# Modulation sums of a three-block transformer kernel: one-hot stationary operand in four column groups, rows turned once a layer

## The chip, the cores and the metric

The kernel runs on one core of one Trainium2 chip. The metric is device time in microseconds (us) of one launch. The engines are TensorE (PE, its weight loads PEld), VectorE (DVE), ScalarE (ACT), GpSimd (POOL) and SyncE (SP), which here only issues weight loads. Everything is float32.

## The reference, cut to what matters

Two transformer layers over 256 tokens and 256 context tokens, then a third block with a mixture of experts. Each of the three layers has a modulation: one or two condition vectors (`c` and `c_ctx` in layers 0 and 1, `c_2` in the third) times a 1024 x 6144 matrix give six vectors that shift, scale and gate the layer.

```python
def modulation(cvec, w, b):
    m = jax.nn.silu(cvec) @ w + b
    return jnp.split(m[..., None, :], 6, axis=-1)
...
        sh1, sc1, g1, sh2, sc2, g2 = modulation(c, w_mod[i], b_mod[i])
        csh1, csc1, cg1, csh2, csc2, cg2 = modulation(c_ctx, w_mod[i], b_mod[i])
        h = x * (1.0 + sc1) + sh1
        hc = xc * (1.0 + csc1) + csh1
```

## The kernel before

Weights come in pieces of 1024 x 512 (2 MB) through a ring of four slots, `wring`, that SP fills in the fixed order `STREAM`; piece i waits until piece i-4 is released. PSUM is eight banks, given out in turn by `claim(name)`: claim i waits until the bank of claim i-8 was freed, and `moved(name)` is the wait for that. Each engine has its own instruction stream, written out by hand, with semaphores between them.

A modulation matrix is 12 chunks of 512 columns, `("mod0", m)` to `("mod2", m)`. The first four chunks of layer 0 are needed at once: `mod_rows` multiplies them on TensorE with the two condition vectors as a stationary operand of two columns, giving rows 2 x 512, which ACT copies to SBUF (`modrow`) and TensorE turns into columns. The eight matmuls of such a chunk accumulate over its eight row blocks k.

The other 32 chunks are spread over the program (`BESIDE`): 8 of layer 0 beside the first projection `ev_in`, 12 of layer 1 and 2 of layer 2 beside the first layer's up projection `up0`, 10 of layer 2 beside `up1`. For such a chunk DVE (`sum_mods`) adds the eight row blocks, each scaled by its entry of the condition vector, into one 128 x 512 tile for each vector; 16 operations with two vectors, 8 with one. What remains is a sum over the 128 partitions. TensorE takes it: a block of 128 x 128 of that tile is the stationary operand, a column of ones the moving one, and the result is a column of 128 values. That is four matmuls for each vector, 208 in all. They stand singly between the matmuls of a `features` or `tokens` call (`take_sum`), one ahead of each of its 128x512 or 128x256 matmuls. ACT copies the 4 or 8 columns to `modc` (`mods`), and `finish_mod` adds the bias on DVE before the layer that needs them.

In the MLP (`mlp`) each block c of `up` is four features of eight matmuls; ACT takes the relu, DVE the square, and DVE sums a chunk after every second square. A chunk summed in block c is taken by TensorE in block c+1, ahead of feature 0 or 2 (`due`).

Every float32 matmul leaves two records in the trace, each with its own weight load; a transpose leaves one. Counts below are of records.

Of the kernel before, what the change touches and what calls it, by code (L numbers as in the profile page):

```python
# [13 lines left out]
P = 128  # L14
# [29 lines left out]
def _place(names):  # L44
    at = 0
    for name, width in names:
# [7 lines left out]
                  ("ones", 1), ("before", P), ("home", NEXP), ("spill", NEXP), ("expert", NEXP), ("turn", SPILLS),  # L54
# [5 lines left out]
def shape_constants():  # L60
# [31 lines left out]
    put("ones", 1.0)  # L92
    put("before", r < t)
# [71 lines left out]
ATT_BANKS = (5, 6, 0, 1, 2, 3, 7, 4)  # L165
# [25 lines left out]
def build(nc, I, out):  # L191
# [10 lines left out]
    with ExitStack() as ctx:  # L202
# [18 lines left out]
        small = sb("small", [P, 592])  # L221
        slot_i = sb("slot_i", [P, 4], I32)
# [37 lines left out]
        modsums = region(tmp, 2560, 2, 2, 512)  # L260

        def modsum(n, v):

            return gtok[:, 2 * (n % 2) + v, 512:D] if SUMMED[n][0] == 0 else modsums[:, n % 2, v, :]

# [173 lines left out]
        csilu_ready = sem("csilu_ready")  # L439
        modc_ready = sem("modc_ready")  # L440
# [110 lines left out]
        def _(pe):  # L551
# [41 lines left out]
            def open_sums(chunk):  # L593

                if chunk is None:
                    return []
                l, m = chunk
                V = vectors(l)
# [51 lines left out]
            def features(name, w, f, lo, hi, chunk=None):  # L650

                sums = open_sums(chunk)
                o = claim(name)
                for k in range(KC):
                    take_sum(sums, k)
# [3 lines left out]
            def tokens(name, w, t, width=512, at=0, chunk=None):  # L659

                sums = open_sums(chunk)
                o = claim(name)
                for k in range(KC):
                    take_sum(sums, k)
# [26 lines left out]
            def mlp(l, tiles):  # L691
                lo = 0
                n = len(tiles) * P
                for c in range(8):
# [3 lines left out]
                    release((f"up{l}", c))  # L698
                for half in range(2):
                    outs = [claim(f"down{l}{half}{t}") for t in tiles]  # L700
                    for g in range(4):
                        w = weights((f"down{l}", 4 * half + g))
                        if half == 0 and g == 0:
                            pe.wait_ge(*moved(f"up{l}31"))
# [103 lines left out]
            def take_alone(chunk):  # L808
                sums = open_sums(chunk)
                for k in range(len(sums)):  # L810
                    take_sum(sums, k)

            for n, c in enumerate(EV_ORDER):
# [7 lines left out]
                elif n == 2:  # L821
                    sums = open_sums(EV_TAKES[(2, 0)])
                    o = claim("lr0")
                    for k in range(KC):
                        take_sum(sums, k)
                        last = mm(o[0:32, :], w[:, k, 0:32], hT[:, k, :], k == 0, k == KC - 1)
                    last.then_inc(bank_full, 1)
                else:
                    for t in range(NT):
# [3 lines left out]
                        if (n, t) == (3, 0):  # L833
                            take_alone(EV_TAKES[(2, 1)])
# [11 lines left out]
                if n < 3:  # L846
                    release(("ev_in", n))
            for t in range(NT):
# [60 lines left out]
            assert count[0] % BANKS == ATT_BANKS[0]  # L909
# [527 lines left out]
        def _(act):  # L1437
# [70 lines left out]
            def mods(chunk):  # L1508

                if chunk is not None:  # L1510
                    l, m = chunk
                    V = vectors(l)
                    move(f"mod{l}_{m}", modc[:, l, 4 * m:4 * m + 4, 0:V],
                         bank(f"mod{l}_{m}")[:, 0:4 * V].rearrange("p (f v) -> p f v", v=V))

# [5 lines left out]
            def relus(l, n):  # L1521

                for i in range(32):
                    mods(due(f"up{l}", i // 4, i % 4))
# [4 lines left out]
            for c in range(4):  # L1529
                move(f"modrow{c}", modrow[0:2, c, :], bank(f"modrow{c}")[0:2, :])  # L1530
# [965 lines left out]
```

## Time and profile before

| | us |
|---|---|
| median of 3 runs (lowest to highest) | 1859.06 (1856.77 to 1860.87) |
| profiled execution, its own time | 1862.66 |
| its span, first to last instruction | 1860.8 |
| PE busy | 1703.6 |
| PE weight loads busy | 908.8 |
| DVE busy | 719.4 |
| ACT busy | 251.4 |

PE is busy in 92% of the span. Weight loads overlap with matmuls, so the two PE rows don't add. A matmul's recorded length includes its way through the pipeline; what it costs the stream is the distance of one start to the next.

### The profile page before, as it was taken

To read this page: it belongs to the slowest core of one execution; us is meant where nothing else is said; L and a number is where in the kernel's file an instruction comes from. 1 tells how busy PE (TensorE), PEld (TensorE's weight loads), DVE (VectorE), ACT (ScalarE), POOL (GpSimd) and SP (SyncE) were. 2 spreads that over 40 slices of the span, in tenths; PEclk is the share of its full clock that TensorE was granted. 3 is DMA by queue.
4 is the path that set the end of the run, shared out by engine and by line. 5 is a ranking of instruction groups with operands and counts; after the bars stand their busy time and mean duration, and the time that the engine had idled before them with its cause. 6 is when DMAs were issued, how large, how long until landed. Compare 5 with 4: busy or idle time off the path is not lost.

```text
span 1860.8 us, 16741 instructions
## 1 busy us (share of the span) xinstructions
PE 1703.6 (92%) x6670; PEld 908.8 (49%) x6670; DVE 719.4 (39%) x1292; ACT 251.4 (14%) x588; POOL 114.0 (6%) x121
## 2 busy tenths in 40 slices
PE   6999999899999999998898999997986675999997
PEld 1445556355554444445564886444744643333332
DVE  0654453557775001023373563012368633111112
ACT  1112113020000000001171110001201311110110
POOL 0000001100000000001000000002022101010001
PEclk9999999999999999999999999998998686999999
DMA  9452150225555322125303687433522127999996
GB/s 348 168 213 91 59 179 26 89 95 200 206 201 205 112 91 91 45 91 220 136 1 113 229 320 276 170 136 79 181 91 92 56 97 282 391 388 390 391 390 253
DMA packets 160685, 334.46 MB, mean 180 GB/s; under 512 B 15192, under 2 KB 15472, under 8 KB 160608
## 3 DMA queue, kind: packets, MB, share of 16 engines
q1 hardware_dynamic: 141408, 298.87, 44.4%
q0 software_dynamic: 18288, 31.37, 5.2%
q10 hardware_dynamic: 912, 3.17, 0.4%
q8 instruction: 53, 0.87, 0.2%
q14 instruction: 24, 0.20, 0.0%
HBM read 355.58 MB, written 15.48 MB: 199 GB/s over the span
## 4 chain that ended last, share of the span: by engine, by line
PE 84%; DVE 9%; DMA 2%; issue 2%; POOL 1%; ACT 1%; SPq 0%; DVEq 0%; ACTq 0%; POOLq 0%
PE psum L570 80%; PE psum L574 4%; POOL small L1329 1%; DMA wring<-in_w_mod 1%; DMA wring<-in_ev_w_in 1%; ACT wide L1460 1%; DVE big L2039 0%; DVE big L1813 0%; DVE small L1880 0%; ACT big L1460 0%; DVE xres L1887 0%; DVE big L2206 0%; DVE big L2225 0%; DVE small L2224 0%; DVE wide L2276 0%
## 5 line engine op out<-in xcount | busy, mean ns | idle before, releaser
L570 PE MATMUL psum<-wring,big 128*128 128x512 f32 (+1 forms) x1536 | 563.4, 603 | 13.5 <-issue 10.2
L570 PE MATMUL psum<-wide,wring 128*128 128x256 f32 (+3 forms) x1648 | 516.5, 478 | 3.5 <-DVE wide L1851 3.5
L570 PEld LDWEIGHTS psum<-wring,big 128*128 128x128 f32 (+1 forms) x1536 | 232.2, 174 | 327.8 <-issue 327.0
L570 PEld LDWEIGHTS psum<-wide,wring 128*128 128x128 f32 (+2 forms) x1648 | 269.2, 182 | 134.3 <-issue 109.0
L570 PE MATMUL psum<-wring,wide 128*128 128x512 f32 (+2 forms) x512 | 210.9, 561 | 3.4 <-DMA wring<-in_ev_w_in 3.4
L1813 DVE SCALAR_TENSOR_TENSOR wide<-wring,csilu,wide 128x512 f32<-128x512 f32 x252 | 175.5, 748 | 3.0
L1865 DVE TENSOR_TENSOR wide<-psum,gate 128x512 f32<-128x512 f32 x28 | 19.4, 691 | 356.7 <-PE psum L570 356.5
L1460 ACT ACTIVATE big<-psum 128x512 f32<-128x512 f32 (+1 forms) x153 | 79.9, 534 | 450.2 <-PE psum L570 394.4
L570 PEld LDWEIGHTS psum<-wring,wide 128*128 128x128 f32 x512 | 92.8, 193 | 89.2 <-issue 83.0
L1329 POOL TENSOR_TENSOR small<-small 128x1 f32<-128x1 f32 (+2 forms) x30 | 40.0, 1334 | 1117.6 <-DVE small L1882 926.6
L570 PE MATMUL psum<-big,wide 128*64 128x512 f32 (+1 forms) x408 | 91.7, 569 | 0.0
L1913 DVE TENSOR_TENSOR big<-big,psum 128x512 f32<-128x512 f32 (+1 forms) x64 | 35.3, 551 | 141.4 <-ACT big L1460 140.9
L570 PEld LDWEIGHTS psum<-const,wide 128*128 128x128 f32 x352 | 62.2, 190 | 55.9 <-issue 53.4
L570 PE MATMUL psum<-big 128*64 128x128 f32 (+5 forms) x608 | 71.2, 348 | 18.0 <-DVE big L2297 7.3
L1460 ACT ACTIVATE wide<-psum 128x256 f32<-128x256 f32 (+3 forms) x108 | 43.3, 415 | 314.3 <-PE psum L574 153.4
L2453 DVE TENSOR_TENSOR wide<-wide,psum 128x256 f32<-128x256 f32 x23 | 9.7, 421 | 180.4 <-ACT wide L1460 180.4
L1813 DVE SCALAR_TENSOR_TENSOR big<-wring,csilu,big 128x512 f32<-128x512 f32 x112 | 74.9, 745 | 0.0
L570 PEld LDWEIGHTS psum<-big 64*128 64x128 f32 (+2 forms) x608 | 51.6, 183 | 26.3 <-issue 13.8
L1460 ACT ACTIVATE wide<-psum,modc 128x256 f32<-128x256 f32 x36 | 18.4, 560 | 325.1 <-PE psum L574 323.5
L574 PE MATMUL psum<-const,wide 128*128 128x128 f32 (+1 forms) x238 | 40.7, 312 | 19.7 <-DVE wide L1905 16.5
L574 PEld LDWEIGHTS psum<-const,wide 128*128 128x128 f32 (+1 forms) x238 | 30.0, 160 | 54.1 <-issue 26.0
L570 PEld LDWEIGHTS psum<-big,wide 128*64 128x64 f32 (+1 forms) x408 | 31.7, 145 | 49.2 <-issue 48.3
(257 smaller groups left out, 1058.5 us busy)
## 6 DMA issues: line engine op xcount, KB each, us to landing
wring<-in_mlp_w SPq DMA_DIRECT2D x32, 2048.0 KB, 8.8
wring<-in_w SPq DMA_DIRECT2D x32, 2048.0 KB, 20.8
wring<-in_w_mod SPq DMA_DIRECT2D x24, 2048.0 KB, 11.9
big<-in_w SPq DMA_DIRECT2D x23, 2048.0 KB, 20.8
wide<-in_w SPq DMA_DIRECT2D x14, 2048.0 KB
wring<-in_w_ada SPq DMA_DIRECT2D x12, 2048.0 KB, 9.2
wring<-in_w_in SPq DMA_DIRECT2D x8, 2048.0 KB, 8.3
wring<-in_ev_w_in SPq DMA_DIRECT2D x6, 2048.0 KB, 13.1
```

The lines of the kernel that those rows point to most:

```text
L570: return nc.tensor.matmul(o, a, b, start=first, stop=last)
L574: return nc.tensor.transpose(o, a, ident[0:n, 0:n])
L1329: nc.gpsimd.tensor_tensor(a, a, half_neg[:, 0:a.shape[1]], ALU.pow).then_inc(rate_done, 1)
L1460: return nc.scalar.activation(o, a, func, **kw)
L1813: ins = v_.scalar_tensor_tensor(acc, w, by, acc, ALU.mult, ALU.add)
L1865: free(v_.tensor_tensor(ubuf, bank(name), gate[:, gv, cs], ALU.mult), name)
L1913: free(v_.tensor_tensor(h, h, bank(name)[:, 0:n], ALU.mult), name)
L2453: v_.tensor_tensor(he[:, i % 2, :], sg[:, i % 2, :], psum[:, i % 2, T:2 * T], ALU.mult).then_inc(he_ready, 1)
```

## The change

The 208 matmuls swap their operands. The stationary operand is now 32 columns of a constant `row`, 63 columns wide with ones in column 31 only, cut so that the ones stand in column m; the moving one is the 128 x 128 block. The result is a row of 128 values in row m of a group of 32 rows, zeros in the other 31; block f goes to row group 32f, so the four blocks of a vector use four column groups of the array. The matmuls of a chunk stand together ahead of the feature (`sum_rows`). DVE adds the 128 x 256 (or 128 x 128) result into a tile of rows of its layer (`add_row`, in place of ACT's copy), and when the layer's last chunk is in, `turn_rows` turns the tile with one matmul for each vector. `finish_mod` adds the bias straight from PSUM.

`mod_rows` is split into four column groups as well: eight row blocks k go to groups k mod 4, with a stationary operand `vec32` of 32 columns (two vectors and zeros), and the turning matmul with the constant `quarter` adds the four groups. PE claims one bank more for each layer, and `ATT_BANKS` is set to fit.

```diff
             def mod_rows():
-                vec = csilu[:, 0:16].rearrange("p (v k) -> p k v", v=2)
+                pe.wait_ge(vec32_ready, 1)
                 for c in range(4):
                     w = weights(("mod0", c))
                     o = claim(f"modrow{c}")
-                    for k in range(KC):
-                        last = mm(o[0:2, :], vec[:, k, :], w[:, k, :], k == 0, k == KC - 1)
+                    for n in range(KC // 4):
+                        for q in range(4):
+                            k = 4 * n + q
+                            last = mm(o[32 * q:32 * (q + 1), :], vec32[:, k, :], w[:, k, :], n == 0, n == KC // 4 - 1)
                     last.then_inc(bank_full, 1)
                     release(("mod0", c))
                 for c in range(4):
                     pe.wait_ge(*moved(f"modrow{c}"))
                     o = claim(f"mod0_{c}")
                     for f in range(4):
-                        last = turn(o[:, 2 * f:2 * f + 2], modrow[0:2, c, f * P:(f + 1) * P])
+                        last = mm(o[:, 2 * f:2 * f + 2], modrow[:, c, f * P:(f + 1) * P], cst("quarter"))
                     last.then_inc(bank_full, 1)
...
-                return [(o[:, f * V + v:f * V + v + 1], modsum(n, v)[:, f * P:(f + 1) * P])
-                        for f in range(4) for v in range(V)]
-
-            def take_sum(sums, k):
-
-                if k < len(sums):
-                    last = mm(sums[k][0], sums[k][1], cst("ones"))
-                    if k == len(sums) - 1:
-                        last.then_inc(bank_full, 1)
+                at = CONST_COLS["row"][0] + 31 - m
+                for v in range(vectors(l)):
+                    for f in range(4):
+                        last = mm(o[32 * f:32 * (f + 1), v * P:(v + 1) * P], const[:, at:at + 32],
+                                  modsum(n, v)[:, f * P:(f + 1) * P])
+                last.then_inc(bank_full, 1)
+
+            def turn_rows(l):
+
+                pe.wait_ge(rows_added, last_row(l))
+                o = claim(f"modT{l}")
+                for v in range(vectors(l)):
+                    last = mm(o[:, v * P:(v + 1) * P], rows_of_layer(l)[:, v, :], ident)
+                last.then_inc(bank_full, 1)
...
+                pe.wait_ge(*moved(f"up{l}31"))
+                turn_rows(l + 1)
                 for half in range(2):
                     outs = [claim(f"down{l}{half}{t}") for t in tiles]
...
+            turn_rows(0)
             for t in range(NT):
                 if t + 1 < NT:
                     scores(t + 1)
...
+            def add_row(chunk):
+
+                l, m = chunk
+                V = vectors(l)
+                name = f"mod{l}_{m}"
+                rows, src = rows_of_layer(l), ready(name)[:, 0:V * P].rearrange("p (v n) -> p v n", v=V)
+                n = SUMMED.index(chunk)
+                if n > 0:
+                    dve.wait_ge(rows_added, n)
+                if chunk == next(x for x in SUMMED if x[0] == l):
+                    ins = v_.tensor_copy(rows, src)
+                else:
+                    ins = v_.tensor_tensor(rows, rows, src, ALU.add)
+                free(ins, name)
+                dve.sem_inc(rows_added, 1)
...
                 for i in range(32):
                     name = f"up{l}{i}"
+                    if due(f"up{l}", i // 4, i % 4) is not None:
+                        add_row(due(f"up{l}", i // 4, i % 4))
                     dve.wait_ge(relu_ready, 32 * l + i + 1)
...
+            signal(v_.memset(vec32, 0.0), vec32_zero)
+            dve.wait_ge(csilu_ready, 1)
+            v_.tensor_copy(vec32[:, :, 0:2], csilu[:, 0:16].rearrange("p (v k) -> p k v", v=2)).then_inc(vec32_ready, 1)
             mods(0, 0, 4)
```

What stands in PE's stream at the start, `mod_rows` between the first two transposes of constants and the transposes of x; before:

```order
L574 MATMUL psum<-const,big 128x96 x2
L570 MATMUL psum<-wring,csilu 2x512 x32
L574 MATMUL psum<-const,wide 128x2 x16
L574 MATMUL psum<-const,xres 128x128 x32
L570 MATMUL psum<-wide,wring 128x512 x32
```

and of the change:

```order
L589 MATMUL psum<-const,big 128x96 x2
L585 MATMUL psum<-wring,wide 32x512 x32
L585 MATMUL psum<-const,wide 128x2 x16
L589 MATMUL psum<-const,xres 128x128 x32
L585 MATMUL psum<-wide,wring 128x512 x32
```

The counts are the same; the output is 32 rows in place of 2, and the 16 small ones are matmuls (L585) where they were transposes (L574).

PE's stream beside `up0`, end of one feature, a chunk's sum and the features after it (`wide,wring` are the features, `const,wide` and `wide,const` the sums); before:

```order
L570 MATMUL psum<-wide,wring 128x512 x9
L570 MATMUL psum<-const,wide 128x1
L570 MATMUL psum<-wide,wring 128x512
L570 MATMUL psum<-const,wide 128x1
L570 MATMUL psum<-wide,wring 128x512
```

and of the change:

```order
L585 MATMUL psum<-wide,wring 128x512 x16
L585 MATMUL psum<-wide,const 32x128 x8
L585 MATMUL psum<-wide,wring 128x512 x16
L585 MATMUL psum<-wide,const 32x128 x8
```

Eight matmuls with one moving column, each ahead of one of the feature's, became eight with 128 moving columns in one piece.

DVE's stream beside `up0`, from one square pair to the next (`big<-big,psum` are the squares, `wring,csilu` the sums over row blocks); before:

```order
L1913 TENSOR_TENSOR big<-big,psum 128x512 x2
L1810 TENSOR_SCALAR wide<-wring,csilu 128x512 x2
L1813 SCALAR_TENSOR_TENSOR wide<-wring,csilu,wide 128x512 x14
L1913 TENSOR_TENSOR big<-big,psum 128x512 x2
L1810 TENSOR_SCALAR wide<-wring,csilu 128x512 x2
```

and of the change:

```order
L1811 SCALAR_TENSOR_TENSOR wide<-wring,csilu,wide 128x512 x14
L1832 TENSOR_TENSOR small<-small,psum 128x256
L1940 TENSOR_TENSOR big<-big,psum 128x512 x2
L1808 TENSOR_SCALAR wide<-wring,csilu 128x512 x2
L1811 SCALAR_TENSOR_TENSOR wide<-wring,csilu,wide 128x512 x14
L1832 TENSOR_TENSOR small<-small,psum 128x256
```

One addition for each chunk (L1832) stands behind the sum and ahead of the next squares.

## Rows read from the trace of the kernel before

**Rows 1.** The page: span, busy time of PE, chain by engine.

```profile
span 1860.8 us, 16741 instructions
...
PE 1703.6 (92%) x6670; PEld 908.8 (49%) x6670; DVE 719.4 (39%) x1292; ACT 251.4 (14%) x588; POOL 114.0 (6%) x121
...
PE 84%; DVE 9%; DMA 2%; issue 2%; POOL 1%; ACT 1%; SPq 0%; DVEq 0%; ACTq 0%; POOLq 0%
```

**Rows 2.** Timeline of PE, first features of `up0`: start, us, form, count, idle before.

```profile
380.86 27.63 PE L570 MATMUL psum<-wide,wring 128*128 128x512 f32 x64
408.33 0.28 PE L570 MATMUL psum<-const,wide 128*128 128x1 f32 x2
...
409.41 0.28 PE L570 MATMUL psum<-const,wide 128*128 128x1 f32 x2
...
423.85 0.28 PE L570 MATMUL psum<-const,wide 128*128 128x1 f32 x2
```

**Rows 3.** Groups of PE by form: all matmuls with one moving column.

```profile
L570 PE MATMUL psum<-const,wide 128*128 128x1 f32 x288 | 40.4, 210 | 0.9 <-issue 0.9
...
L570 PE MATMUL psum<-const,big 128*128 128x1 f32 x128 | 18.3, 220 | 0.0
```

**Rows 4.** Timeline of PE, forms in one and in two column groups.

```profile
218.70 1.97 PE L570 MATMUL psum<-big,lnb 128*64 128x128 f32 x32
220.60 1.09 PE L574 MATMUL psum<-const,big 128*128 128x128 f32 x8
...
873.90 13.98 PE L570 MATMUL psum<-wring,wide 128*128 128x256 f32 x64
887.81 7.13 PE L570 MATMUL psum<-wide,wring 128*64 128x256 f32 x64
```

**Rows 5.** Timeline of PE beside `ev_in`.

```profile
113.46 0.38 PE L570 MATMUL psum<-const,big 128*128 128x1 f32 x2
...
114.75 0.38 PE L570 MATMUL psum<-const,big 128*128 128x1 f32 x2
...
126.00 8.83 PE L570 MATMUL psum<-wring,wide 128*128 128x512 f32 x16 [3.44 <-DMA wring<-in_ev_w_in]
134.66 1.84 PE L570 MATMUL psum<-const,big 128*128 128x1 f32 x16
136.43 6.45 PE L570 MATMUL psum<-gate 33*128 33x512 f32 x8
```

**Rows 6.** Timeline of PE at the start of the program.

```profile
13.93 8.91 PE L570 MATMUL psum<-wring,csilu 128*2 128x512 f32 x16 [6.60 <-DMA wring<-in_w_mod]
...
24.38 20.76 PE L570 MATMUL psum<-wring,csilu 128*2 128x512 f32 x48 [1.54 <-DMA wring<-in_w_mod]
...
45.07 1.21 PE L574 MATMUL psum<-const,wide 2*128 2x2 f32 x16
...
51.91 27.70 PE L570 MATMUL psum<-wide,wring 128*128 128x512 f32 x64 [1.99 <-DVE wide L1851]
```

**Rows 7.** Windows: busy of each engine, granted clock, DMA share, GB/s.

```profile
33.00:36.00 3.00, 3.00 (x9) 0.59 (x8) 0.00 (x0) 0.00 (x0) 0.00 (x0) 1.00 1.05 386
...
138.00:140.00 2.00, 2.00 (x3) 0.67 (x2) 0.00 (x0) 0.89 (x2) 0.00 (x0) 0.50 1.05 387
```

**Rows 8.** DMA issues of the page: size of one chunk.

```profile
wring<-in_w_mod SPq DMA_DIRECT2D x24, 2048.0 KB, 11.9
```

**Rows 9.** Timeline of SP: issue of the load that PE waits for.

```profile
112.78 0.58 SPq L1245 DMA_DIRECT2D wring<-in_ev_w_in  x1
```

**Rows 10.** Timeline of DVE in `up0` and `up1`.

```profile
410.01 0.88 DVE L1810 TENSOR_SCALAR wide<-wring,csilu 128x512 f32<-128x512 f32 x2
...
420.08 0.68 DVE L1913 TENSOR_TENSOR big<-big,psum 128x512 f32<-128x512 f32 x1
...
1030.94 0.42 DVE L1913 TENSOR_TENSOR big<-big,psum 128x256 f32<-128x256 f32 x1 [3.03 <-ACT big L1460]
```

**Rows 11.** Timeline of PE: matmuls with the identity as moving operand.

```profile
301.77 3.74 PE L570 MATMUL psum<-const,modc 128*128 128x128 f32 x32
```

More of the change, by code:

```diff
@@ L53 @@
                   ("win0", P), ("win1", P), ("pick", 4),
-                  ("ones", 1), ("before", P), ("home", NEXP), ("spill", NEXP), ("expert", NEXP), ("turn", SPILLS),
+                  ("ones", 1), ("quarter", 2), ("row", 63), ("before", P), ("home", NEXP), ("spill", NEXP), ("expert", NEXP), ("turn", SPILLS),
                   ("late", LATE * SLOTS)])
@@ L92, in shape_constants @@
     put("ones", 1.0)
+    put("quarter", (r % 32) == np.arange(2)[None, :])
+    put("row", np.arange(63)[None, :] == 31)
     put("before", r < t)
@@ L260, in build, with rows_of_layer, last_row @@
         modsums = region(tmp, 2560, 2, 2, 512)
+        vec32 = region(tmp, 2048, KC, 32)
         def modsum(n, v):
             return gtok[:, 2 * (n % 2) + v, 512:D] if SUMMED[n][0] == 0 else modsums[:, n % 2, v, :]
+        def rows_of_layer(l):
+            return region(small, 176, 2, P) if l < 2 else modrows[:, :].unsqueeze(1)
+        def last_row(l):
+            return max(n for n, (x, _) in enumerate(SUMMED) if x == l) + 1
         carried = region(tmp, 2560, 6, 512)
@@ L650, in features @@
             def features(name, w, f, lo, hi, chunk=None):
-                sums = open_sums(chunk)
+                sum_rows(chunk)
                 o = claim(name)
                 for k in range(KC):
-                    take_sum(sums, k)
                     last = mm(o[:, 0:hi - lo], w[:, k, f * P:(f + 1) * P], hT[:, k, lo:hi], k == 0, k == KC - 1)
@@ L659, in tokens @@
             def tokens(name, w, t, width=512, at=0, chunk=None):
-                sums = open_sums(chunk)
+                sum_rows(chunk)
                 o = claim(name)
                 for k in range(KC):
-                    take_sum(sums, k)
                     last = mm(o[:, 0:width], hT[:, k, t * P:(t + 1) * P], w[:, k, at:at + width], k == 0, k == KC - 1)
@@ L806, in outputs @@
                                 last.then_inc(bank_full, 1)
[L808 to L811, printed above, removed]
             for n, c in enumerate(EV_ORDER):
@@ L908, in _ @@
                 pe.wait_ge(bank_freed[b], (count[0] - 1 - b) // BANKS + 1)
-            assert count[0] % BANKS == ATT_BANKS[0]
+            assert all((count[0] + n) % BANKS in ATT_BANKS[0:4] for n in range(2)), count[0] % BANKS
             def logits1(s, j):
@@ L1529, in _ @@
             for c in range(4):
[L1530 removed]
+                move(f"modrow{c}", modrow[:, c, :])
             modulate("mix0")
@@ L1552, in _ @@
             decays("ret", exp_ret, 0)
-            for i in range(2):
-                mods(EV_TAKES[(2, i)])
             for t in range(NT):
@@ L1932, in _ @@
             signal(last, laret_ready)
-            for c, j in ((0, 0), (0, 1), (1, 0), (1, 1)):
-                sum_mods("ev_in", c, j)
+            sum_mods("ev_in", 0, 0)
+            sum_mods("ev_in", 0, 1)
+            sum_mods("ev_in", 1, 0)
+            add_row((0, 4))
+            sum_mods("ev_in", 1, 1)
+            add_row((0, 5))
             dve.wait_ge(mix0_in, 80)
@@ L1937, in _ @@
             sum_mods("ev_in", 2, 0)
+            add_row((0, 6))
             def keep_v(c, t):
@@ L1943, in _ @@
             keep_v(1, 0)
+            add_row((0, 7))
             heads = lambda a: a.rearrange("p (h n) -> p h n", h=4)
@@ L2001, in _ @@
             keep_v(1, 1)
+            add_row((0, 8))
             dve.wait_ge(*moved("cumret"))
@@ L2027, in _ @@
                 keep_v(4, t - 1)
+                if t == 2:
+                    add_row((0, 9))
             keep_v(4, 3)
@@ L2033, in _ @@
             states(2)
+            add_row((0, 10))
             states(3)
+            add_row((0, 11))
             def keep(name, dst, mask, n=4):
```

52 lines of the change are left out of this document (26 added, 26 removed).

## The prediction, made before the change was run

> **What bounds the kernel now.** I read the page first: PE is busy in 1703.6 of 1860.8 us and makes up 84% of the chain that ended last [rows 1]. So an instruction taken off PE shortens the program wherever PE does not then wait for something else. Next come the groups by form. The matmuls with one moving column have 288 + 128 = 416 records [rows 3], which is 52 vectors x 4 matmuls x 2 records, the 208 sums. Their mean of 210 ns says little, since it includes the pipeline; what they cost the stream must be read from starts.
>
> The timeline of PE in the first MLP gives that. The 64 feature records from 380.86 to 408.33 take 27.47 us, 0.429 each. From 408.33 to 409.41, one sum matmul and one feature matmul take 1.08 us, so the sum matmul costs 1.08 - 0.86 = 0.22 us. From 408.33 to 423.85, two features and one chunk of eight sums take 15.52 us; less 32 x 0.429 = 13.73 that is **1.79 us a chunk of two vectors** [rows 2]. A chunk of one vector has half, 0.90. The cost is about the same where eight stand alone: 16 records from 134.66 to 136.43, 1.77 us [rows 5]. I read it as the load of 128 stationary columns that a one-column matmul is too short to cover.
>
> **The sums in their new form.** The trace has no run of 32-column groups, so I bound it. The nearest row is the one with 64 stationary columns and 128 moving ones, whose outputs alternate between two column groups: 32 records from 218.70 to 220.60, 59 ns each. With all 128 stationary columns in use, 32 records with 128 moving ones take 3.74 us, 117 ns each [rows 4, 11]. So two groups do overlap, and the 256-column forms say the same: 64 records in 13.91 us in one group and in 7.1 us in two [rows 4]. I take 59 ns for four groups too: both records of a matmul go to the same group and stand next to each other, so if starts keep their order only two are ever in flight. Upper bound 117 (no overlap), lower bound 30 (four in flight).
>
> Changing the form costs something. Beside `lr0`, whose features use 32 columns, a pair takes 1.29 us (113.46 to 114.75) against 1.08 [rows 2, 5]; two changes cost 0.21, so 0.1 each. A chunk now stands in one piece and pays two. New price: 16 x 0.059 + 0.2 = **1.15 us with two vectors, 8 x 0.059 + 0.2 = 0.67 with one**. Gain 0.64 and 0.23.
>
> The Trainium skill ("TensorEngine Tiling (Array Packing)", Tiling Modes) lists 128x32 as four independent tiles and says that changing the mode drains the engine; the lr0 pair agrees with the second half. By its "Up to 4x" a record could cost 30 ns; "TensorE: Matmul & The Clock Gate" (Part 1) gives some 62 ns of sequencer time per matmul, which would hold four groups at what two show. The sum above needs neither.
>
> How many chunks are on the path? Twelve of two vectors and two of one beside `up0`, ten of one beside `up1`: PE has no wait there. Beside `ev_in` there are eight of two vectors. One of them (lr0's) lies ahead of a wait of 3.44 us for a weight load [rows 5]; what it saves is waited out again. The two before it count, since that load is issued at 112.78, when their piece is released [rows 9], and so comes earlier by what was saved before. Sum: 19 x 0.64 + 12 x 0.23 = **14.9 us**.
>
> **The start.** The four first chunks run in one group: 48 records from 24.38 to 45.07, 0.43 each, 6.9 us a chunk [rows 6]. The loads are faster: the DMA engines are full at 386 GB/s [rows 7], 2048 KB [rows 8] are 5.4 us. Chunk 1 is what PE waited for until 24.38, so chunks 2 and 3 are in by 29.8 and 35.2. In two-way overlap a chunk takes 3.4 us, and `mod_rows` ends at 38.6 in place of 45.0: 6.4 saved. Against that the 16 turning transposes, 1.15 us, become 16 matmuls of 32 records with 128 stationary and two moving columns; by the run at 134.66, 111 ns each, that is 3.55 us, 2.4 more, and the modulation of x waits for them. The next weights are in by then (40.6), one load behind chunk 3. PE now stands idle between chunks; the clock read 0.50 at 138 us, after the wait at 126.00 and the short sums [rows 5, 7], so I take 0.8 off for part of a chunk at half clock. Net **3.2 us**. If four ran at once, 1.7 more.
>
> **What is added.** `turn_rows`: two matmuls (four records) in layers 0 and 1, one in layer 2, at 117 ns [rows 11]: 0.47, 0.47, 0.23. They stand where PE has nothing else, behind the wait for the last square, ahead of `down` (and ahead of `scores(1)`), so they count in full; with one longer addition in `finish_mod` **1.5 us lost**. The waits in front of them are old ones, or met long before.
>
> `add_row` on DVE: 32 operations from PSUM of at most 0.42 us (128x256) [rows 10]. Behind each stand the squares, and behind the squares the bank that PE claims eight claims later. Per block of `up0` DVE has two sums of 10.07 us (410.01 to 420.08), four squares of 0.7 and now two additions: 23.8 us of 29.8. The sum that ends at 420.08 is wanted at 423.85, and with the change at 408.33 + 1.15 + 13.73 = 423.2; 3.1 us are left, so the additions stay covered. If that cover went, each microsecond beyond it would cost PE one per block, seven in all. ACT loses 32 copies on which nothing waits.
>
> **Sum.** 14.9 + 3.2 - 1.5 = 16.6 us. The profiled execution has 1862.66 us (span 1860.8); the median of the runs is 3.6 lower, and the sum goes to it: 1859.06 - 16.6 = **1842.5 us**.
>
> **Rivals.**
> *Waits and clock take back the start* (0.22). After lr0 PE waits 3.44 us now; lr0 itself gets shorter by 2.3 (eight pairs of 1.29 become 1.15 and 6.86), so it will stand still for some 5.7. The granted clock was 0.50 in stretches behind this place [rows 7]; features at 126.00 took 8.66 us where 6.86 is full speed, and those of the 33-row matmuls behind 6.39 for eight records, 0.8 each in place of 0.43 [rows 5]. If a longer stand adds another 3.4 us of lost time and the start's 3.2 go the same way, 10 us are left: 1849. For it: PE is fed in shorter bursts. Against it: the long run of one-column matmuls at 134.66, after which the clock fell, is replaced by denser work, and the 5 us lost there could even come back.
> *Four groups at once* (0.10). 30 ns a record takes another 0.47 and 0.24 off each chunk: 19 x 0.47 + 12 x 0.24 = 11.8, and 1.7 at the start: 30 us gained, 1829. The tiling page's factor is this case. Against it: no row of any small matmul is below 59 ns.
> *The groups of 32 don't overlap* (0.07), the slower side. Then a record costs 0.112, a chunk 16 x 0.112 + 0.2 = 2.0 against 1.79 (1.1 against 0.90 with one vector), the start gains nothing and pays 2.4 for the turning: 19 x 0.2 + 12 x 0.2 + 2.4 + 1.5 = 10 us slower, 1869. With start and turning as forecast (+1.7), the sums decide from 1.86 us a chunk, 104 ns a record. Against it: both two-group rows.
>
> **How the numbers follow.** The forecast case (0.61) has its own range, 1838 to 1847: 0.1 us either way in the form change over 31 chunks, and the start from 1 to 5. The range for all is 1831 to 1852; it takes in most of the first rival and stops short of the second and third. A difference of 0.2% is 3.7 us, about what this kernel's measurement can tell from none. Faster by more: the forecast, the second, and nearly all of the first rival: 0.90. Within 0.2%: 0.03. Slower: 0.07.
>
> **What would show it.** In the changed trace: 16 records of form 128*32 with 128 moving columns in 0.95 us between two features; 13.7 us from a chunk's end to the next chunk's start in `up0`, and 14.9 from start to start; the last `mod_rows` matmul near 38.6 and the first 128x512 feature near 48.5 (now 51.91); the wait for `in_ev_w_in` up from 3.4 to between 5 and 6 us and ended near 121; no wait of PE for DVE L1811 in `up0`. The prediction is wrong if records of the new form are 0.1 us apart or more, if they are 0.03 apart, or if PE runs at half clock for more than 10 us in the first 150.

## The result and the profile after

| us | before | after |
|---|---|---|
| median (lowest to highest) | 1858.25 (1856.77 to 1860.87), 4 runs | 1829.94 (1828.41 to 1835.35), 4 runs |
| profiled execution, its own time | 1862.66 | 1828.41 |

The ratio is 0.9848, 95% interval 0.9829 to 0.9867: 28.3 us faster, where 16.6 were forecast. The forecast range, 1831 to 1852, does not hold it; the rival "four groups at once", given 0.10 and 1829 us, does.

The page of the changed kernel: span, busy time, chain by engine [rows 1].

```profile
span 1826.6 us, 16792 instructions
...
PE 1653.0 (90%) x6696; PEld 865.7 (47%) x6696; DVE 731.2 (40%) x1328; ACT 246.0 (13%) x556; POOL 114.3 (6%) x121
...
PE 81%; DVE 9%; DMA 5%; issue 2%; POOL 2%; ACT 1%; SPq 1%; DVEq 0%; POOLq 0%; ACTq 0%
```

PE lost 50.6 us of busy time, more than the program lost: recorded lengths include the pipeline, and DMA's share of the chain rose from 2% to 5%. So starts are needed again. The timeline of PE beside `up0`, over two chunks, answers to [rows 2]:

```profile
395.48 0.64 PE L585 MATMUL psum<-wide,const 128*32 128x128 f32 x16
396.05 14.00 PE L585 MATMUL psum<-wide,wring 128*128 128x512 f32 x32
409.98 0.65 PE L585 MATMUL psum<-wide,const 128*32 128x128 f32 x16
```

From one chunk to the next are 14.50 us. The 32 feature records are 13.73 at 0.429 each, so a chunk of two vectors costs **0.77 us**, against 1.79 before and 1.15 forecast. Beside `up1`, where a chunk has one vector:

```profile
1012.53 0.43 PE L585 MATMUL psum<-wide,const 128*32 128x128 f32 x8 [0.23 <-issue]
...
1019.99 0.43 PE L585 MATMUL psum<-wide,const 128*32 128x128 f32 x8
```

7.46 us from chunk to chunk, where the trace of before has 7.80: 0.34 saved, 0.23 forecast. Groups of PE by form, against [rows 3].

```profile
L585 PE MATMUL psum<-wide,const 128*32 128x128 f32 x288 | 12.8, 280 | 1.7 <-DMA wring<-in_mlp_w 0.9 <-issue 0.7
```

Their mean of 280 ns is above the 210 of before, although they cost the stream less than half. A mean length says nothing of a price where records overlap.

The start, timeline of PE [rows 6]:

```profile
25.92 3.64 PE L585 MATMUL psum<-wring,wide 128*32 128x512 f32 x16 [7.18 <-DMA wring<-in_w_mod]
31.35 3.64 PE L585 MATMUL psum<-wring,wide 128*32 128x512 f32 x16 [1.78 <-DMA wring<-in_w_mod]
36.77 1.92 PE L585 MATMUL psum<-wring,wide 128*32 128x512 f32 x16 [1.78 <-DMA wring<-in_w_mod]
38.62 3.82 PE L585 MATMUL psum<-const,wide 128*128 128x2 f32 x32
42.31 5.26 PE L589 MATMUL psum<-const,xres 128*128 128x128 f32 x32
49.35 2.81 PE L585 MATMUL psum<-wide,wring 128*128 128x512 f32 x6 [1.78 <-DVE wide L1876]
```

A chunk now takes 1.85 us where 6.9 were needed (the two of 3.64 ran at about half the clock: the granted clock reads 0.56 from 30 to 36 us). So each chunk is done before the next one's load is in, and `mod_rows` ends at 38.62 instead of 45.07, although in this execution the first chunk could start only at 15.47, 1.54 us later than in the trace of before [rows 6]. Turning takes 3.69 instead of 1.15, and the transposes of x behind it, 3.71 before, take 5.26. The first feature starts at 49.35, 2.6 us earlier. The windows of this stretch (columns as in [rows 7]) show why the transposes were slow:

```profile
38.00:42.00 4.00, 4.00 (x39) 3.38 (x31) 0.50 (x3) 0.60 (x1) 0.00 (x0) 1.00 1.05 386
42.00:46.00 4.00, 4.00 (x24) 4.00 (x24) 1.60 (x6) 1.81 (x4) 0.00 (x0) 0.57 1.05 388
```

The granted clock was 0.57 of full speed at 42 to 46 us, mostly at the lower of its two levels, 1.2 of 2.4 GHz. Beside `ev_in`, timeline of PE [rows 5]:

```profile
122.25 9.71 PE L585 MATMUL psum<-wring,wide 128*128 128x512 f32 x16 [7.08 <-DMA wring<-in_ev_w_in]
131.89 0.65 PE L585 MATMUL psum<-big,const 128*32 128x128 f32 x16
132.46 3.70 PE L585 MATMUL psum<-gate 33*128 33x512 f32 x8
136.09 7.13 PE L585 MATMUL psum<-wring,wide 128*128 128x512 f32 x16
```

The wait for the load grew from 3.44 to 7.08 us and ends at 122.25, 3.75 earlier than before. The features behind it are slower (9.64 us, was 8.66), but the 33-row matmuls take 3.63 in place of 6.39 and the features behind them 7.06 in place of 9.25. From the end of the load's wait to the end of these features PE needed 26.07 us before and needs 20.90 now. Of these 5.17 us 1.02 is what the sum has for the chunk in between (1.79 less 0.77), so 4.2 us came back here that the sum did not have.

`turn_rows` ahead of `down0` and `down1`:

```profile
599.72 0.71 PE L585 MATMUL psum<-const,small 128*128 128x128 f32 x4 [1.54 <-DVE big L1940]
...
1117.67 0.49 PE L585 MATMUL psum<-const,modrows 128*128 128x128 f32 x2 [1.06 <-DVE big L1940]
```

The next matmul starts 0.55 and 0.32 us behind them; with 0.53 for layer 0 they cost 1.4.

The sum for the two profiled executions, made at the first transposes of the third block (1268.05 before, 1240.06 after): 19 chunks x 1.02 = 19.4, 12 x 0.34 = 4.1, the start 1.7 (2.6 less 0.9: the load that ends the wait was issued 4.59 us earlier, at 108.19, and landed only 3.75 earlier), the clock near 130 us 4.2, `turn_rows` -1.4. That is 28.0, and 27.99 are measured. Behind this place nothing was changed. The profiled executions part by another 6.2 us there, and the medians (28.3) do not; it is taken for chance here, and no run tests it. That 28.0 and 28.3 lie so close is luck in part: the four runs of the changed kernel range over 6.9 us.

### The profile page after: what moved, and what is told of

The parts are those of the page before. It is cut to its first block, busy times and chain, and to the rows that moved or that the text cites. A ratio compares the mean times of both kernels' runs of the same rounds, so it can differ in the third digit from the quotient of the medians.

```text
span 1826.6 us, 16792 instructions
## 1 busy us (share of the span) xinstructions
PE 1653.0 (90%) x6696; PEld 865.7 (47%) x6696; DVE 731.2 (40%) x1328; ACT 246.0 (13%) x556; POOL 114.3 (6%) x121
## 4 chain that ended last, share of the span: by engine, by line
PE 81%; DVE 9%; DMA 5%; issue 2%; POOL 2%; ACT 1%; SPq 1%; DVEq 0%; POOLq 0%; ACTq 0%
PE psum L585 77%; PE psum L589 4%; DMA wring<-in_w_mod 1%; POOL small L1343 1%; DMA wring<-in_mlp_w 1%; DMA wring<-in_ev_w_in 1%; DMA y_slots<-lnb 1%; ACT wide L1474 1%; DVE big L2080 0%; SPq L1259 0%; DVE small L1905 0%; ACT big L1474 0%; DVE xres L1912 0%; DVE big L2247 0%; DVE big L2266 0%
## 5 line engine op out<-in xcount | busy, mean ns | idle before, releaser
L585 PE MATMUL psum<-wring,big 128*128 128x512 f32 (+1 forms) x1536 | 559.8, 598 | 9.5 <-issue 8.9
L585 PE MATMUL psum<-wide,wring 128*128 128x256 f32 (+3 forms) x1648 | 484.3, 470 | 3.3 <-DVE wide L1876 3.3
L585 PEld LDWEIGHTS psum<-wring,big 128*128 128x128 f32 (+1 forms) x1536 | 231.3, 173 | 320.1 <-issue 319.1
L585 PEld LDWEIGHTS psum<-wide,wring 128*128 128x128 f32 (+2 forms) x1648 | 278.6, 181 | 194.4 <-issue 168.2
L585 PE MATMUL psum<-wring,wide 128*128 128x512 f32 (+3 forms) x576 | 216.1, 595 | 26.0 <-DMA wring<-in_w_mod 18.9
L1890 DVE TENSOR_TENSOR wide<-psum,gate 128x512 f32<-128x512 f32 x28 | 19.4, 691 | 355.5 <-PE psum L585 355.4
L585 PEld LDWEIGHTS psum<-wring,wide 128*128 128x128 f32 (+1 forms) x576 | 96.9, 187 | 134.2 <-issue 108.8
L585 PE MATMUL psum<-big,wide 128*64 128x512 f32 (+1 forms) x408 | 91.4, 568 | 0.0
L1474 ACT ACTIVATE wide<-psum 128x256 f32<-128x256 f32 (+2 forms) x108 | 43.4, 416 | 322.5 <-PE psum L589 148.9
L585 PE MATMUL psum<-big 128*64 128x128 f32 (+5 forms) x608 | 68.5, 343 | 18.0 <-DVE big L2338 7.9
L585 PEld LDWEIGHTS psum<-big 64*128 64x128 f32 (+2 forms) x608 | 48.4, 176 | 26.4 <-issue 13.0
L589 PE MATMUL psum<-const,wide 128*128 128x128 f32 x222 | 39.4, 320 | 19.7 <-DVE wide L1930 16.6
L585 PEld LDWEIGHTS psum<-big,wide 128*64 128x64 f32 (+1 forms) x408 | 31.5, 144 | 49.2 <-issue 48.3
L589 PEld LDWEIGHTS psum<-const,wide 128*128 128x128 f32 x222 | 28.9, 162 | 52.9 <-issue 25.1
L589 PE MATMUL psum<-const,big 128*128 128x128 f32 (+1 forms) x212 | 32.3, 301 | 23.0 <-DMA big<-in_b_ada 6.8
```

Source lines behind the costliest of these rows:

```text
L585: return nc.tensor.matmul(o, a, b, start=first, stop=last)
L589: return nc.tensor.transpose(o, a, ident[0:n, 0:n])
L1474: return nc.scalar.activation(o, a, func, **kw)
L1890: free(v_.tensor_tensor(ubuf, bank(name), gate[:, gv, cs], ALU.mult), name)
```

## The experiments

The theory after the result: the four column groups work at the same time, so a record costs 0.03 us and not 0.06; and what the clock gave back near 130 us came with the end of the run of one-column matmuls there. The rival for the first: the gain came from standing the sums together, or from their order.

**micro: the forms by themselves.** All of the kernel's computation is left out; runs of 64 records (32 for 512 columns) stand between six records of 128x512. Each line gives the name of the run, the stationary columns (FULL 128, HALF 64, QUARTER 32), the column group of each matmul in turn, and the moving columns.

```python
    ("full", FULL, [0] * 32, 128),
    ("halves", HALF, [0, 1] * 16, 128),
    ("quarters", QUARTER, [0, 1, 2, 3] * 8, 128),
    ("twos", QUARTER, [0, 0, 1, 1, 2, 2, 3, 3] * 4, 128),
    ("eights", QUARTER, [0] * 8 + [1] * 8 + [2] * 8 + [3] * 8, 128),
    ("one_quarter", QUARTER, [0] * 32, 128),
    ("two_quarters", QUARTER, [0, 1] * 16, 128),
    ("narrow_quarters", QUARTER, [0, 1, 2, 3] * 8, 32),
    ("wide_quarters", QUARTER, [0, 1, 2, 3] * 4, 512),
```

> This kernel leaves the whole computation out: it only issues matmuls of float32 with constant operands and writes zeros. Each section has 32 matmuls (64 records) of 128 moving columns, told apart by the name of their stationary tensor, twice over. Theory A (each column group runs on its own, all four at once): one group alone (one_quarter) about 107 ns a record, the same as 128 stationary columns; two groups in turn (halves, two_quarters) 54 to 59; four in turn (quarters) 27 to 30. Theory B (the narrow stationary is what is cheap, groups don't matter): one_quarter 30 ns too. Theory C, my forecast's (a record waits for the one before it in its group and starts keep their order): two matmuls of a group next to each other (twos) or eight (eights) cost far more than quarters, some 80 to 100 ns; if each group works off its own queue, twos stay near 30 and only eights grow.

Timeline of PE, the second operand names the run:

```profile
16.87 7.31 PE L69 MATMUL psum<-moving,st_full 128*128 128x128 f32 x64
24.01 2.74 PE L62 MATMUL psum<-moving,sep 128*128 128x512 f32 x6
26.68 3.71 PE L69 MATMUL psum<-moving,st_halves 128*64 128x128 f32 x64
30.33 2.84 PE L62 MATMUL psum<-moving,sep 128*128 128x512 f32 x6
33.10 1.96 PE L69 MATMUL psum<-moving,st_quarters 128*32 128x128 f32 x64
34.98 2.84 PE L62 MATMUL psum<-moving,sep 128*128 128x512 f32 x6
37.76 2.02 PE L69 MATMUL psum<-moving,st_twos 128*32 128x128 f32 x64
39.71 2.84 PE L62 MATMUL psum<-moving,sep 128*128 128x512 f32 x6
42.48 5.95 PE L69 MATMUL psum<-moving,st_eights 128*32 128x128 f32 x64
48.37 2.84 PE L62 MATMUL psum<-moving,sep 128*128 128x512 f32 x6
51.14 7.17 PE L69 MATMUL psum<-moving,st_one_quarter 128*32 128x128 f32 x64
58.24 2.84 PE L62 MATMUL psum<-moving,sep 128*128 128x512 f32 x6
...
67.41 0.76 PE L69 MATMUL psum<-moving,st_narrow_quarters 128*32 128x32 f32 x64
68.10 2.84 PE L62 MATMUL psum<-moving,sep 128*128 128x512 f32 x6
```

From a run's start to the start of what follows, over 64 records: one full group 7.14 us, 112 ns each; two groups 3.65, 57 ns; four groups 1.88, **29 ns**; two matmuls to a group before the next 1.95, 30 ns; eight to a group 5.89, 92 ns; one group of 32 alone 7.10, 111 ns. The second round of the same runs gives 1.89 us in turn and 7.11 for one group. So a group alone is as slow as the full array, and groups overlap, two in a row as well. Only long runs to one group lose it: two matmuls in a row cost nothing, eight nearly all. That each group works off a short queue of its own would explain this; the run shows the times and not the queue. With 512 moving columns four groups take 3.57 / 32 = 112 ns a record (full 429). With 32 moving columns a record in four groups costs 0.69 / 64 = 11 ns.

The Trainium skill ("TensorEngine Tiling (Array Packing)", Theoretical Speedup) gives up to 4 times for groups of 32; the run agrees, 7.14 / 1.88 = 3.8. The figure that the prediction set against it, some 62 ns for each matmul, stands in the Trainium skill ("TensorE: Matmul & The Clock Gate", Part 1) only for hardware decode switched off, a condition that the prediction left out and no run here shows. It did not hold a record at 59 ns: 29 were measured, and the narrow run took 22 ns for a matmul of two records.

**fmajor: the order within a chunk.** The loops over blocks and vectors are exchanged, so that two matmuls in a row go to one group.

```diff
-                for v in range(vectors(l)):
-                    for f in range(4):
+                for f in range(4):
+                    for v in range(vectors(l)):
```

> The changed kernel with the two vectors' matmuls of one column group next to each other (four records in a row in each group) in place of a round over the four groups. Group queues: a chunk stays at 0.77 us between features (14.50 us from chunk to chunk in the first MLP), the whole within 0.2%. Starts in order: the same group's four records stand behind each other, a chunk costs about 1.4 us, 20 chunks x 0.65 = 13 us slower than the changed kernel, near 1843.

Beside `up0` (timeline of PE):

```profile
400.50 0.66 PE L585 MATMUL psum<-wide,const 128*32 128x128 f32 x16
401.10 14.00 PE L585 MATMUL psum<-wide,wring 128*128 128x512 f32 x32
```

0.60 us from a chunk's start to the feature's, where the changed kernel has 0.57. The order in pairs costs next to nothing here either, as group queues had it, and not the 0.65 more a chunk that starts in order would cost. The one time, 1834.72 us, lies in the spread of the changed kernel; its start is read below.

**spread: the new matmuls one by one**, each ahead of one matmul of the feature, as the old ones stood.

```diff
-                sum_rows(chunk)
+                sums = open_rows(chunk)
                 o = claim(name)
                 for k in range(KC):
+                    take_row(sums, k)
```

> The changed kernel with its row matmuls spread again, one ahead of each matmul of the feature, so only the piece-wise place differs. If overlap between groups and one change of form per chunk make the gain, each spread matmul pays two changes of form (0.2 us by the lr0 pair of before) and its own two records alone (0.2): 8 x 0.4 = 3.2 us a chunk against 0.77, and some 20 x 2.4 + 12 x 1.2 = 62 us slower than the changed kernel, near 1892. If the new operand roles alone make the gain, it stays within 5 us of the changed kernel.

1916.78 us median of 4 (1909.63 to 1919.4), ratio 1.0294 (1.0263 to 1.0325): 56 us slower than before, 84 slower than after_again below (62 were expected). The chunk beside `lr0` and the one that stands alone behind it stay in one piece. Timeline of PE beside `up0`:

```profile
420.95 0.41 PE L585 MATMUL psum<-wide,const 128*32 128x128 f32 x2
421.29 1.13 PE L585 MATMUL psum<-wide,wring 128*128 128x512 f32 x2
422.34 0.41 PE L585 MATMUL psum<-wide,const 128*32 128x128 f32 x2
```

A pair of new and feature matmul takes 1.39 us, so a single new matmul costs 0.53. Two records alone in one group are 0.22, which leaves 0.31 for two changes of form: 0.15 each by this estimate, not the 0.1 of the prediction. The block agrees: 16 x 0.029 + 2 x 0.15 = 0.76, 0.77 measured. Eight single ones are 4.2 us against 0.77, 3.5 more in 18 chunks and 1.6 in 12: 82, where 84 were measured.

**together: the old matmuls in one piece** ahead of the feature, operands as before.

```diff
                 sums = open_sums(chunk)
+                for k in range(len(sums)):
+                    take_sum(sums, k)
                 o = claim(name)
                 for k in range(KC):
-                    take_sum(sums, k)
```

> The kernel before with its one-column matmuls standing together ahead of each feature; nothing else is changed. If the place mattered, it would gain; by the run of 16 records that stood alone before (1.77 us) a chunk stays at 1.8 us and the time within 0.2% of before. The rival: the load of the first weights behind a one-column matmul was paid at each of eight places and is now paid once, up to 8 us faster; or long runs of one-column matmuls lower the granted clock, and it is slower by several us.

1860.52 us (1857.43 to 1862.42), ratio 0.9999 (0.9989 to 1.0009). The place alone gives nothing (the eight beside `lr0` stayed single); with spread it shows that the new form needs to stand together and the old one does not care.

**after_again, oldstart, early: the parts of the start.** The changed kernel once more; the changed kernel with the old `mod_rows` and turning; and the changed kernel with each chunk turned as soon as it is summed:

```diff
                     release(("mod0", c))
-                for c in range(4):
                     pe.wait_ge(*moved(f"modrow{c}"))
```

> The changed kernel once more, as the base for the three beside it: 1826 to 1836. If the clock's fall over the 33-row matmuls in the first 150 us is gone for a reason, they take 3.7 us here too; if it was chance, 6.4.

> The changed kernel with the four first chunks multiplied and turned as before (one group of two columns, 16 transposes); the 32 other chunks stay in the new form. Theory: the start is worth what the first feature's start moved, 2.6 us, so it is 2 to 3 us slower than the changed kernel, 1832.5; rival: at half clock behind the idle start the split gains nothing, same time; or later DMA waits swallow it.

> The changed kernel with each first chunk turned right behind its own matmuls, while PE waits for the next chunk's load, in place of all four turned at the end. Of 32 records only the last 8 stand behind the last chunk, plus the wait for ACT's copy of 0.7 us: 3.7 us shrink to 1.6, so 2.1 us faster than the changed kernel if the DMA wait later lets it through, which takes up to 1 of it. Rival: no gain, since the modulation of x waits for something else or the clock falls with the idle time.

| | median (lowest to highest) | ratio (95%) | first feature of the profiled run |
|---|---|---|---|
| after_again | 1832.51 (1827.59 to 1836.05) | 0.9861 (0.9842 to 0.9880) | 48.50 |
| oldstart | 1832.92 (1832.55 to 1833.26) | 0.9856 (0.9841 to 0.9872) | 52.33 |
| early | 1828.19 (1826.63 to 1835.5) | 0.9843 (0.9823 to 0.9862) | 47.39 |

Between these medians the new start is worth 0.4 us, although it brings the first feature 3.8 us forward in the profiled executions. The median of the changed kernel's first four runs, 1829.94, would make it 3.0, so its worth is known no better than that. Turning early, expected to be 2.1 us faster, is 4.3 below after_again, but the intervals overlap. The spread tells more: oldstart stays within 0.7 us, the new start ranges over 8.5. The profiled execution of fmajor, whose start is the same code, shows another case of it (timeline of PE):

```profile
38.83 6.99 PE L585 MATMUL psum<-const,wide 128*128 128x2 f32 x32
45.68 6.12 PE L589 MATMUL psum<-const,xres 128*128 128x128 f32 x32
53.52 6.67 PE L585 MATMUL psum<-wide,wring 128*128 128x512 f32 x15 [1.72 <-DVE wide L1876]
```

Turning takes 6.85 us instead of 3.69, and the first feature starts at 53.52, later than in the kernel before. It is no rarity: the profiled executions with this code at the start have their first feature at 48.50, 49.35, 51.02 (swap, below), 51.47 (spread), 53.43 (onecol, below) and 53.52. The granted clock reads 0.50 from 38 to 50 us in fmajor's; its first four:

```profile
38.00:42.00 4.00, 4.00 (x23) 3.17 (x16) 0.17 (x1) 0.60 (x1) 0.00 (x0) 0.50 1.05 387
```

In oldstart PE works without a break from 25 to 45 us and the clock reads 1.00 up to 50. In the new start it stands in a wait for each chunk's load, and where the lower clock then falls varies: in the changed kernel's trace on chunks that wait for their loads anyway and on part of the transposes of x, in fmajor's on the turning and all the transposes as well, which are on the path. That this explains the runs without a trace is inferred from their spread, not shown.

**onecol: one-column matmuls put back.** Nothing of the computation is left out; eight one-column matmuls, whose results nobody reads, stand ahead of the chunk's sum before the 33-row matmuls, where before had its run of eight.

```diff
+                for f in range(pad):
+                    mm(o[:, 256 + f:257 + f], modsum(n, f // 4)[:, (f % 4) * P:(f % 4 + 1) * P], cst("ones"))
...
-                            sum_rows(EV_TAKES[(2, 1)])
+                            sum_rows(EV_TAKES[(2, 1)], pad=8)
```

> The changed kernel with the eight one-column matmuls of before (16 records, 1.77 us) put back ahead of one chunk's row matmuls beside ev_in, just ahead of the 33-row matmuls; their results go to columns that nobody reads. If such a run is what lowered the granted clock there, the slow stretch is back: 1.8 us for itself and 3 to 5 us for half clock, so 5 to 7 us slower than the changed kernel. If the stretch was chance or came from the 33-row matmuls themselves, 1.8 us slower.

1834.6 us (1832.89 to 1841.33), ratio 0.9863 (0.9847 to 0.9879). The median is 2.1 us above that of after_again, inside both spreads; that is what the rival expected (1.8), not the 5 to 7 of the theory. The profiled execution is the slowest of the four, 1841.33, with the slow stretch in it (timeline of PE):

```profile
136.52 1.84 PE L585 MATMUL psum<-const,big 128*128 128x1 f32 x16
138.29 0.64 PE L585 MATMUL psum<-big,const 128*32 128x128 f32 x16
138.86 6.71 PE L585 MATMUL psum<-gate 33*128 33x512 f32 x8
145.50 9.16 PE L585 MATMUL psum<-wring,wide 128*128 128x512 f32 x16
```

The 33-row matmuls take 6.64 again (after 3.63, before 6.39) and the features behind them 9.10 (7.06, 9.25). The closest trace without the run is fmajor's, whose first feature starts at 53.52 (here 53.43) and whose wait for the load is 7.38 us (7.36):

```profile
137.30 3.70 PE L585 MATMUL psum<-gate 33*128 33x512 f32 x8
140.92 7.13 PE L585 MATMUL psum<-wring,wide 128*128 128x512 f32 x16
```

It has full speed there and is 6.6 us faster: 1.8 for the run itself and 5.0 for the two groups. Whether the clock fell in onecol's other three runs (1832.89 to 1835.07) no trace shows; their times lie inside the changed kernel's own range.

**before_again: the same place in the kernel before, once more.**

> The kernel before, unchanged, for a second look at the clock around the run of eight one-column matmuls at 126 to 150 us. Theory (the run of one-column matmuls at 134.66 us brings back the half clock): the 33-row matmuls take about 6.5 us again at 136 us, and the eight-group features behind them over 8.6 us. Rival (chance of that execution): 3.7 us. Time 1858 us.

```profile
137.24 1.84 PE L570 MATMUL psum<-const,big 128*128 128x1 f32 x16
139.01 4.28 PE L570 MATMUL psum<-gate 33*128 33x512 f32 x8
...
143.23 9.89 PE L570 MATMUL psum<-wring,wide 128*128 128x512 f32 x16
```

The one run took 1860.57 us. The 33-row matmuls take 4.22 and not 6.5: here the expectation was off. The features behind them take 9.73, as expected (over 8.6). So the lower clock comes after the run of one-column matmuls, a little sooner or later: these features are slow in all four traces that have the run (before, before_again, together, onecol), and at full clock in five of the six that lack it and keep the order of loads (after, after_again, oldstart, early, fmajor). The exception is spread, where they take 8.76 us at 144.29 without such a run. (The runs with the exchange of loads below have a stand of PE ahead of these features and do not count here.) So the lower clock goes with the run of one-column matmuls; that the run brings it about is likely, it is not the only cause, and ten traces are few.

**swap, early_swap, oldstart_swap: the load that PE waits for.** Its 7.08 us wait ends with an `ev_in` tile whose transfer stands behind that of chunk m8. The two are exchanged, in the changed kernel, in early and in oldstart:

```diff
+        if name == "ev_in":
+            at = s.index(("mod0", 8))
+            s[at:at + 2] = [s[at + 1], s[at]]
         return s
```

> The changed kernel with two neighbours in the order of loads exchanged: the fourth ev_in tile is issued ahead of the mod chunk m8 instead of behind it. Nothing is left out. Theory A (TensorE's wait of 7.08 us that ends at 122.25 us is one transfer of some 5.4 us too long, since chunk m8's transfer stands ahead of the tile's): the wait falls to about 1.5 us, the matmuls with 33 rows start near 127 instead of 132.46, VectorE's sum of m8 moves some 5.4 us later without making TensorE wait, and the median is 1827 us, ratio 0.983. Rival B (the sum of m8 comes too late, and VectorE's copies of ev_in's results wait behind it): the wait moves to a later tile and the median stays at 1831 to 1833.

> The run before with one more edit: each of the four chunks of the first mod rows is turned as soon as it is summed, while TensorE waits for the next chunk's load. Nothing is left out. If the start's turning lies in idle time and the load order pays as theory A says, the two add: 1823 us, ratio 0.981. If either is taken back by the other (the tile is then awaited longer, since it is issued when a slot comes free and needs its 5.4 us of transfer), 1826 to 1828.

> The changed kernel with the first mod rows summed and turned as before the change, and the two loads exchanged as in the two runs before. Nothing is left out. Theory A (the start's split gives a time that depends on the clock the turning gets, 48.5 to 53.5 us at the first feature against 52.3 here): first feature at 52.3, median 1828, within 1.5 us of the run swap, with a narrower spread than it. Rival: the exchange makes the start's gain show, and this run is 4 us behind swap.

| | median (lowest to highest) | ratio (95%) |
|---|---|---|
| swap | 1830.32 (1828.3 to 1836.42) | 0.9846 (0.9826 to 0.9867) |
| early_swap | 1827.18 (1825.79 to 1827.79) | 0.9820 (0.9805 to 0.9835) |
| oldstart_swap | 1832.9 (1832.49 to 1834.53) | 0.9854 (0.9836 to 0.9872) |

The wait went where the rival said, to a later place, and theory A's gain did not come; the median of swap lies between the two forecasts. Timeline of PE in swap:

```profile
118.49 7.13 PE L588 MATMUL psum<-wring,wide 128*128 128x512 f32 x16 [1.65 <-DMA wring<-in_ev_w_in]
...
126.13 3.70 PE L588 MATMUL psum<-gate 33*128 33x512 f32 x8
134.49 8.62 PE L588 MATMUL psum<-wring,wide 128*128 128x512 f32 x16 [4.67 <-DVE small L1835]
```

The wait for the load fell to 1.65 us as expected, and one of 4.67 us for DVE now ends 16 us later. The timeline of DVE says what is late:

```profile
124.75 9.36 DVE L1814 SCALAR_TENSOR_TENSOR big<-wring,csilu,big 128x512 f32<-128x512 f32 x14
134.02 0.41 DVE L1835 TENSOR_TENSOR small<-small,psum 128x256 f32<-128x256 f32 x1
```

Chunk m8 now lands last, its sum fills DVE until 134, and `add_row`, which frees a PSUM bank, stands behind it. In the features behind that wait the clock is down again (8.55 us; granted clock 0.78 from 134 to 142 us). Of the 5.4 us of transfer hardly anything is left: the median of swap lies between the two of the changed kernel, oldstart_swap equals oldstart, and early_swap is 1.0 us below early, inside the intervals. Theory A had oldstart_swap at 1828 and within 1.5 us of swap: it is 2.6 behind, though with the narrower spread that was expected. early_swap fits the case that one gain takes back the other (1826 to 1828). Of all versions early_swap has the lowest median: 32 us faster than before, and 2.8 to 5.3 below the two medians of the changed kernel. Its five runs lie within 2.0 us.

## Why the prediction was wrong

- **The price of a record, the step that failed.** "both records of a matmul go to the same group and stand next to each other, so if starts keep their order only two are ever in flight": the premise of order did not limit these runs. Pairs in one group ran at 30 ns a record, and 29 was measured in turn, not 59. Chunks cost 0.77 and 0.56 us in place of 1.15 and 0.67. That is 19 x 0.38 + 12 x 0.11 = 8.5 of the 11.7 us by which the gain was underrated; the clock near 130 us is 4.2, the start takes 1.5 off again (1.7 for 3.2). The lower bound of 30 was in the text; the two-group rows [rows 4] were taken as the nearest row although they cannot tell two groups from four.
- **The form change** was 0.15 us and not 0.1. The 0.21 for two [rows 2, 5] was read from pairs with a one-column matmul in them; that this matmul costs the same beside 32 stationary columns as beside 128 was assumed, and no run tests it. It took 0.1 us a chunk from the gain of the step above.
- **The one-column price**, 1.79 us a chunk, and the count of 31 chunks on the path held: the sum for the two profiled executions closes with them.
- **The start**, forecast at 3.2. Its end at 38.6 was right and its working was not: chunk 3 landed at 36.77, not 35.2 (in this execution the first two chunks already came 1.54 us later than in the trace of before), and took 1.85, not 3.4. Turning cost 2.5 more, as forecast (2.4). The clock was given 0.8 us and cost between 1.5 (the transposes of x in this trace) and 5.6 in fmajor's (3.2 in the turning, 2.4 in the transposes). Against oldstart the whole start is worth 0.4 or 3.0 us of median, by which of the two medians of the changed kernel is taken.
- **The wait for the load**: forecast 5 to 6 us ended near 121, measured 7.08 ended at 122.25.
- **The clock near 130 us**, 4.2 us, was named in the prediction as something that "could even come back" and left out of the sum. The trace of onecol has it with the run of one-column matmuls, its median hardly shows it, and spread shows that the clock can fall there without it: the run is the likely cause, not a shown one. That these 4.2 us made the rival's 1829 come out so exactly is luck; its own sum had 1.7 more from the start, which did not come, and none of these 4.2.
- **What was added** held: `turn_rows` 1.4 (forecast 1.5), additions of 0.42 us on DVE, and no wait of PE for DVE's sums in `up0`.
- **The rival of waits and clock** (1849) had its mechanism right in one half: the stand before the load grew and the features behind it lost 1 us. More came back behind them than was lost.
- **The signs.** "0.03 apart" came true. So did "half clock for more than 10 us in the first 150": by the windows of the trace I estimate 27 us, waits included. But the same estimate gives 14 for the kernel before, so this sign could not tell the cases apart.

## What to carry to other kernels

If a TensorE operand has only a few columns, put it in groups of 32 and send neighbouring matmuls to different groups: in float32 with 128 columns of moving data four groups cost a quarter of one here, if the matmuls stand together. Alone between matmuls of another form each pays two changes of form, and the same operands are then slower than what they replace. Read the price from starts, and where no row has the form itself, measure a bare run of it before choosing between bounds a factor of two apart.

A transfer brought forward delays its neighbour in the queue: look at who waits for that one, and at what stands behind them, before counting the gain. And work that TensorE finishes sooner than its loads arrive turns into short stands, after which the clock may be down for what is on the path.

## What the runs showed of the hardware that was not expected

- Four column groups take 128 moving float32 columns in 29 ns a record and 32 columns in 11 ns; a group alone takes 111 at 128 columns, the same as the full array's 112. Two matmuls in a row to one group cost nothing (30 ns), eight do (92 ns).
- A change between 128*128 and 128*32 costs about 0.15 us, an estimate from two sets of starts (spread, and the chunk of 0.77 us).
- The same code at the start ran its turning in 3.7 us (changed kernel) or in 6.9 (fmajor and onecol), with the granted clock at 1.00 or 0.50 in 38 to 42 us.
- Behind a run of eight one-column matmuls, at most 1.8 us long, the features were slow in four traces of four (8.5 to 9.7 us instead of 7.06), without it in one of six.
